# Modulation loads of a two-layer block spread over four stages instead of two

## The reference, cut to what matters

```python
c_act = jax.nn.silu(c)
for l in range(DEPTH):                      # DEPTH = 2
    mod = (c_act @ ada_w[l] + ada_b[l])[:, None, :]
    sh1, sc1, g1, sh2, sc2, g2 = jnp.split(mod, N_MOD, axis=-1)
    h = rms_norm(x, norm1_w[l]) * (1.0 + sc1) + sh1
    x = x + g1 * hybrid_mixer(h, w_in[l], w_out[l], ...)
    h = rms_norm(x, norm2_w[l]) * (1.0 + sc2) + sh2
    x = x + g2 * conv_ffn(h, w_gate[l], w_val[l], conv_w[l], conv_b[l], w_down[l])
return rms_norm(x, final_norm_w)
```

## Time and profile before

| | us |
|---|---|
| median of 3 runs | 4075.55 |
| lowest and highest of the 3 | 4073.48 and 4076.36 |
| the profiled execution, its own time | 4080.34 |
| its span in the trace | 4078.5 |
| granted TensorE clock, mean share of full | 0.978 |

### The profile page before, as it was taken

How to read it: one execution, slowest core, us unless ns; L and a number is a source line. 1 busy time by engine, 2 the same in 40 slices (tenths; PEclk the granted TensorE clock), 3 DMA queues, 4 the chain that set the end, 5 groups by cost and what they waited for, 6 DMA issues and landing times.

```text
span 4078.5 us, 69709 instructions
## 1 busy us (share of the span) xinstructions
PE 3851.0 (94%) x28924; PEld 3114.1 (76%) x28924; DVE 2019.9 (50%) x3575; ACT 1742.9 (43%) x2569; POOL 801.1 (20%) x1120
## 2 busy tenths in 40 slices
PE   8898999999899999999999999998999999989997
PEld 5676788777688877878777778876777788768885
DVE  4675662127543127256663466225545555356603
ACT  4365222347533247355553332235645554342223
POOL 1112222221222221200001222221120000222221
PEclk9899999999999999999999999999999999999998
DMA  9846998984589974833224789986573222779995
GB/s 311 245 104 128 291 286 187 203 181 106 119 186 193 190 165 111 188 72 68 68 64 97 168 181 195 190 179 143 114 174 68 62 57 55 155 155 194 190 194 133
DMA packets 191756, 628.98 MB, mean 154 GB/s; under 512 B 22993, under 2 KB 28369, under 8 KB 191057
## 3 DMA queue, kind: packets, MB, share of 16 engines
q0 software_dynamic: 160704, 549.53, 62.2%
q1 hardware_dynamic: 28176, 70.79, 5.0%
q10 hardware_dynamic: 2560, 4.20, 0.4%
HBM read 612.89 MB, written 2.10 MB: 151 GB/s over the span
## 4 chain that ended last, share of the span: by engine, by line
PE 48%; ACT 6%; DVE 5%; DMA 2%; issue 1%; SPq 0%; DVEq 0%; ACTq 0%; POOL 0%
PE bank L228 11%; PE bank L230 11%; PE bank L229 11%; PE bank L2081 6%; ACT gate L2241 1%; PE bank L1767 1%; PE bank L2044 1%; ACT L2241 1%; PE bank L2070 1%; DVE rw_z L2503 1%; PE bank L1749 1%; PE bank L1740 1%; ACT acc L2241 1%; DMA at_sw<-at_raw 1%; ACT w_lo L161 1%
## 5 line engine op out<-in xcount | busy, mean ns | idle before, releaser
L228 PE MATMUL bank<-h_hi,w_hi 128*128 128x512 f32 x2608 | 1068.2, 410 | 37.5 <-DMA w_lo<-in_b_wup 12.5
L230 PE MATMUL bank<-h_hi,w_lo 128*128 128x512 f32 x2608 | 1025.4, 393 | 0.0
L229 PE MATMUL bank<-h_lo,w_hi 128*128 128x512 f32 x2608 | 1024.8, 393 | 0.0
L161 ACT ACTIVATE w_lo<-w_hi 128x1024 fp32r<-128x1024 f32 (+2 forms) x558 | 557.0, 1002 | 1017.6 <-DMA w_hi<-in_a_wgv 297.3
L228 PEld LDWEIGHTS bank<-h_hi,w_hi 128*128 128x128 f32 x2608 | 495.1, 190 | 171.6 <-issue 54.8
L229 PEld LDWEIGHTS bank<-h_lo,w_hi 128*128 128x128 f32 x2608 | 495.9, 190 | 106.6 <-issue 11.3
L230 PEld LDWEIGHTS bank<-h_hi,w_lo 128*128 128x128 f32 x2608 | 494.7, 190 | 107.3
L2241 ACT ACTIVATE gate<-bank 128x512 f32<-128x512 f32 x96 | 57.3, 597 | 274.2 <-PE bank L2081 274.1
L228 PE MATMUL bank<-fb_y_hi,w_hi 128*128 128x512 f32 x352 | 137.2, 390 | 0.4 <-DMA w_lo<-in_b_wd 0.4
L228 PE MATMUL bank<-fa_y_hi,w_hi 128*128 128x512 f32 x352 | 137.0, 389 | 0.4 <-DMA w_lo<-in_a_wd 0.4
L230 PE MATMUL bank<-fb_y_hi,w_lo 128*128 128x512 f32 x352 | 137.0, 389 | 0.0
(11 more groups left out here) (462 smaller groups left out, 7566.3 us busy)
## 6 DMA issues: line engine op xcount, KB each, us to landing
w_hi<-in_a_wgv POOLq DMA_DIRECT2D x80, 512.0 KB, 5.6
w_lo<-in_a_wgv POOLq DMA_DIRECT2D x80, 512.0 KB, 7.7
w_hi<-in_b_wup POOLq DMA_DIRECT2D x80, 512.0 KB, 5.2
w_lo<-in_b_wup POOLq DMA_DIRECT2D x80, 512.0 KB, 7.4
w_hi<-in_a_wh POOLq DMA_DIRECT2D x48, 512.0 KB, 4.9
w_lo<-in_a_wh POOLq DMA_DIRECT2D x48, 512.0 KB, 5.6
fa_ada_raw<-in_ada SPq DMA_DIRECT2D x48, 512.0 KB, 8.2
w_hi<-in_b_wrkv POOLq DMA_DIRECT2D x48, 512.0 KB, 4.6
```

Source lines behind the costliest of these rows:

```text
L161: st.do(st.eng.activation(self.lo[:, s], self.hi[:, s].bitcast(F32), ACT.Copy, scale=-1.0), (self.neg_made, n + 1))
L228: pe.matmul(out, self.hi[:, a], hh[:, k0 + k, :], start=first and k == 0, stop=False)
L229: pe.matmul(out, self.hi[:, a], hl[:, k0 + k, :], start=False, stop=False)
L230: mm = pe.matmul(out, self.lo[:, a], hh[:, k0 + k, :], start=False, stop=last and k == ks - 1)
```

## The change

The work stays the same in kind and amount: 80 loads, 20 groups behind the prologue. It is divided otherwise:

| stage | loads before | loads after | groups after |
|---|---|---|---|
| mixer, layer 0 | 32 | 24 | 4 to 9 of layer 0 |
| feed-forward, layer 0 | 48 | 32 | 10 and 11 of layer 0, 0 to 5 of layer 1 |
| mixer, layer 1 | 0 | 16 | 6 to 9 of layer 1 |
| feed-forward, layer 1 | 0 | 8 | 10 and 11 of layer 1 |

Each feed-forward now makes the `g2` that it multiplies by at its own end. In the mixer of layer 0 the 16 loads after the early ones are added at 4 in a section (two at u = 0, one each at u = 1 and 2) instead of 6 (two each); in the mixer of layer 1 at 2 in a section (places 0, 1, 3, 4, 6, 7, 9, 10). In the feed-forwards 2 loads are added in a block instead of 3, in blocks 0 to 15 and 0 to 3. Products come behind projections 0, 0, 3, 6, 9, 12 in the first mixer (before: 0, 0, 2, 4, 6, 8, 10, 12) and 0, 0, 5, 11 in the second.

```diff
@@ mixer_a
-        ada = Ada(sc, run, [io["ada"][0, g, d] for g in range(4, 12) for d in range(4)]) if l == 0 else None
+        groups = range(4, 10) if l == 0 else range(6, 10)
+        ada = Ada(sc, run, [io["ada"][l, g, d] for g in groups for d in range(4)])
...
         def ada_at(d):
 
-            return (d - EARLY) // 2
+            return (d - EARLY) * 3 // (2 if l else 4)
...
-            if ada:
-                pe.wait_ge(mods_kept, 1)
+            pe.wait_ge(mods_kept, 1)
...
-                if ada and G == 5:
+                if G == 5:
                     dve.wait_ge(ada.used, ada.groups)
                     st.settle()
-                    at = A_AT["ada_b"][0]
-                    st.do(dve.tensor_tensor(mods[:, 0, 16:48], banks[7][:, 0:32], par[:, at + 16:at + 48], ALU.add),
-                          (mods_kept, 1))
+                    at, first, count = A_AT["ada_b"][0], 4 * groups[0], 4 * ada.groups
+                    st.do(dve.tensor_tensor(mods[:, l, first:first + count], banks[7][:, 0:count],
+                                            par[:, at + first:at + first + count], ALU.add), (mods_kept, 1))
@@ ffn_a
-        ada = Ada(sc, run, [io["ada"][1, g, d] for g in range(12) for d in range(4)], 3, raw, 4) if l == 0 else None
+        groups = [(l, 10), (l, 11)] + [(1, g) for g in range(0 if l else 6)]
+        ada = Ada(sc, run, [io["ada"][i, g, d] for i, g in groups for d in range(4)], 3, raw, 2 if l else 4)
...
         def ada_at(d):
 
-            return d // 3
+            return d // 2
...
-            if ada:
-                dve.wait_ge(ada.used, ada.groups)
-                st.settle()
-                at = A_AT["ada_b"][0]
-                st.do(dve.tensor_tensor(mods[:, 1, :], banks[7][:, 0:48], run.par_a[:, 1, at:at + 48], ALU.add))
+            dve.wait_ge(ada.used, ada.groups)
+            st.settle()
+            at = A_AT["ada_b"][0]
+            st.do(dve.tensor_tensor(mods[:, l, 40:48], banks[7][:, 0:8], par[:, at + 40:at + 48], ALU.add))
+            if l == 0:
+                st.do(dve.tensor_tensor(mods[:, 1, 0:24], banks[7][:, 8:32], run.par_a[:, 1, at:at + 24], ALU.add))
```

More of the change, by code:

```diff
@@ L809, in _ @@
             sp.dma_start(reset[:, :], io["a_reset"]).then_inc(const_in, 16)
-            for d in range(ada.steps if ada else 0):
+            for d in range(ada.steps):
                 ada.load(sp, d)
@@ L1101, in _ @@
                     ws.project(pe, banks[i % 2][:, :], hh, hl, between=between)
-                    for g in range(ada.groups if ada else 0):
+                    for g in range(ada.groups):
                         if max(ada_at(4 * g + 3), -1) + 1 == i:
@@ L1295, in _ @@
             st.do(dve.tensor_scalar(omlb[:, :], lbt[:, :], -1.0, 1.0, ALU.mult, ALU.add), (par_made, 1))
-            for d in range(EARLY if ada else 0):
+            for d in range(EARLY):
                 ada.add(st, d)
@@ L1418, in _ @@
             sc.enter_and_clear(sp)
-            if ada:
-                for d in range(ada.steps):
-                    ada.load(sp, d)
+            for d in range(ada.steps):
+                ada.load(sp, d)
             if rope:
```

## The result

The changed kernel took 4050.95 us (median of 4 runs, 4046.7 to 4051.45), the kernel before 4075.95 beside it (4 runs, 4073.48 to 4076.36). The ratio is 0.9941 with a 95% interval of 0.9929 to 0.9953, so the gain is 24 us (19 to 29). The prediction was 4069.5 us, a gain of 6. The sign was forecast, the size was not.

What follows compares the result with a forecast made beforehand. The prediction took TensorE, working in 94% of the span, to bound the kernel. Its terms -11, -7, +7.6 and +4.4 summed to -6.0 us, from a median of 4075.55 to 4069.5 us, range 4059 to 4080.

Steps and rivals of the forecast that it cites:

- First mixer: Layer 0 mixer, 32 to 24 loads and 8 to 6 groups: forecast to gain 11.2 us, taken as -11.
- upper bound of 22.8: First mixer, sections 0 to 3: largest gain in us if nothing but products remained, leaving 104.3 us.
- the replay: VectorE's in-order work in the first mixer, stepped through with measured durations to find which TensorE instructions wait next.
- the residue: First mixer, sections 0 to 3: 11.6 us of gaps, lower clock and late rotations still left after the change.
- gap at the scores of head 0: First mixer: scores due at 109.5, second rotation ready at 113.3; a 3.8 us gap replaces the product's 5.6.
- mask gap in section 3, with its clock: First mixer: value product waits 2.9 us for its mask in section 3, plus 1 us of lower clock.
- First feed-forward: Layer 0 feed-forward, 48 to 32 loads: four products less, -3.6, and fewer weight waits, -3.3; together -7 us.
- Second mixer: Layer 1 mixer, 0 to 16 loads: products +3.6, value projections +3, small gaps +1; together +7.6 us.
- rival (c): Second mixer's scores and value products fall behind VectorE in all four sections: +28 there, sum +14.6, 4090 us; chance 0.05.
- Second feed-forward: Layer 1 feed-forward, 0 to 8 loads: products +1.8, first weight wait +1.8, other loads 0.8; together +4.4 us.
- (b): First mixer's gaps go altogether, -20 there with the rest as forecast: sum -15, 4060.5 us; chance 0.2.
- (a): Each load costs its old average, 1.02 us in mixers, 0.45 in feed-forwards: sum +4.6, 4080 us; chance 0.2.

Runs made afterwards that it cites:

- the small loads: Kernel before, but modulation loads after those that first fill the slots bring 8 of 512 columns; additions and products stay: 4036.65 us, ratio 0.9914.
- the two versions with 24: Changed kernel with eight loads moved from first feed-forward to second mixer (24 each), with two or three load slots in the mixers: ratios 0.995 and 0.9946.
- three slots: Kernel before with three slots instead of two for the first mixer's loads, same loads in the same places: 4059.85 us, ratio 0.9973.

## Why the prediction was wrong

**First mixer, forecast -11, measured -17.4. This is the step that failed.** The upper bound of 22.8 and the floor of 104.3 us were near: TensorE is busy 104.70 us of the 109.26. The order of the replay was right as well. The gap of the product went, nothing waits for a product, the scores of head 0 are late next, and section 2's mask is late behind its pair (in the first of two executions). The stretch with sections 0 to 3 was forecast near 116 us and took 109.3 and 109.0. What failed is the residue, the time that the replay left in gaps and lower clock: 11.6 us forecast, 109.26 - 104.3 = 5.0 measured (4.7 in the second execution). Term by term:

| term of the residue | forecast | first execution | second |
|---|---|---|---|
| gap at the scores of head 0 | 3.8 | 1.48 | 2.07 |
| lower clock behind it | 2 | none | 1.4 |
| mask gap in section 2 | 1.6 | 0.88 | none |
| mask gap in section 3, with its clock | 2.9 + 1 | none | none |
| rotations late elsewhere | 1.3 | 1.32 | 0.18 |

(In the first execution 0.33 at section 1's mask, 0.55 of waiting for weights and 1.4 of longer busy time come on top; the forecast's 1.0 for the second mixer's own gap goes off.)

Two terms make nearly all of the difference, the scores of head 0 and the mask of section 3.

*Head 0.* The replay had the second transfer of the swap landed at 111.1, the rotation ready at 113.3 and TensorE there at 109.5. In the changed kernel that transfer (line 960, now 961) is issued at 104.0:

```profile
DMA to landing us min/median/max: 7.0/7.0/7.0
```

So it lands at 111.0 and the rotation ends at 113.1, as forecast; but TensorE gets there at 113.28 - 1.48 = 111.8. It began its first head projection 1.4 us later (89.92 against 88.50), and so the swap was issued 1.4 later too. Counted from that start, the landing is shorter by 1.5 us (7.0 for 8.5) and TensorE is later by 0.9, 0.55 of it a wait for weights. Together they turn 3.8 into 1.4. The 1.5 us are not shown to be the change's work. The loads up to here are the same ones before and after, and this transfer took 8.5, 7.3 and 7.8 us in three executions of the kernel before, 7.0 and 7.9 in two of the changed one. The forecast stood on the longest of the five.

*Section 3.* The prediction gives 2.9 + 1 without its working. The second load of this pair, issued at 162.4, landed sooner than the 6.2 of the earlier trace rows:

```profile
DMA to landing us min/median/max: 5.0/5.0/5.0
```

In the second execution it took 3.9 us. The swap that VectorE needs ahead of it (second rotation of section 2, issued at 154.0) took 4.5, and 4.6 in the second execution, where the median of the earlier trace rows is 6.6. My estimate from these rows: with 6.6 and 6.2 in place of 4.5 and 5.0 the load would be issued at 164.5, landed at 170.7 and added at 172.2, and the first mask made at 172.9, while the value product was due at 170.4. That is 2.5 us, near the forecast's 2.9. At this place landings were short whenever the loads were added four to a section: this swap took 4.5 to 5.2 us in seven executions, and 4.2 to 8.0 in six at six to a section.

Transfers in general did not become shorter. All second transfers of swaps in the first mixer, after the change:

```profile
DMA to landing us min/median/max: 4.5/6.7/7.5
```

The median is 6.7 here and 6.5 in the second execution; before it was 6.6, 5.9 and 6.6 in three executions. The loads issued from 100 to 191 us have medians of 6.0 and 6.0 after, and 6.2, 6.2 and 5.4 before. So a replay with one median for every transfer of a kind was wrong at single places and not by a common factor. The 5.3 us that it gives the swap of section 1 stand in no row; that swap took 7.0 and 4.8.

What did change is how long VectorE stands waiting for loads: 24.6, 18.7 and 23.0 us from 84 to 210 us in three executions of the kernel before, 10.0 and 13.1 in the changed one. With landings of the same length, I put this down to the larger distance between one addition and the next. That bytes in flight cause the gaps is shown by the small loads (332.9 us with all additions in place), and that the pace has a part of its own by six a section (339.6 against 334.2 with the same 24 loads). How much of the 6.4 us by which the forecast was off is the change's work and how much is scatter of single transfers stays open.

**The lower clock.** I took 2 us behind a gap of 3.8 and 1 behind 2.9. In the first execution, with gaps of 1.48 us at most, the clock stayed at its upper level, and the 8.1 us that I had put down to the clock went nearly whole: the stretch reads 1.00. In the second execution of the changed kernel the mechanism did show, smaller: a gap of 2.07 us ahead of the scores of head 0, and then eight matmuls in 3.82 us that take 2.39 otherwise:

```profile
114.20 3.82 PE L1012 MATMUL bank<-ma_rot 128*128 128x512 f32 x8 [2.07 <-DVE ma_rot L1202]
```

That is 1.4 us in place of 2, in a first mixer that still took 334.1. So a gap's price is its length plus what follows it, if anything does.

**First feed-forward, forecast -7, measured -9.2.** Four products less account for 3.6 at 0.9 each. The weight waits fell by 4.9 us in the trace (8.6 to 3.7), where I had said 3.3, and 0.7 is left over. The bound of -11 held. The choice of "perhaps a third" of the waits was a guess, and the rows had no better; most of the waits went, those at the start stayed, as said.

**Second mixer, forecast +7.6, measured +4.6.** The four products are there: sections 0 to 3 grew by 102.48 - 98.93 = 3.55 us, forecast 3.6. The value projections grew by 1.7 us, not 3: they took 46.94 against 45.23. I had carried over the difference between the first mixer and the second, less 1.5 for the chip's slow start. No run shows that 1.5. The first mixer's value projections take 51.63 us with the same eight loads, 4.7 more than these, so the difference between the two mixers is mostly something else and no measure of loads. The small gaps (+1) did not come; the slack of 2.66 us at the mask held. The stage's clock is 0.98, so rival (c) is out.

**Second feed-forward, forecast +4.4, measured +2.5.** Two products, 1.8, and 0.7 for the weight waits at the start, where I had 1.8 and 0.8.

**Sum.** The four terms were off by 6.4, 2.2, 3.0 and 1.9 us, all in one direction, 13.5 in all. No one cause for all four is shown. The first is the residue above, the third the value projections, and the second and fourth are no larger than the 2.3 us by which a feed-forward differs between executions of one kernel. The other 5 us are the difference between -19.5 in the stages of five executions and 24 by the medians, which is within the interval.

**Rivals.** (b), that the first mixer's gaps go altogether, was nearest to what happened: -17.4 where it said -20. It had 0.2; and even it kept the second mixer at +7.6 and gave 4060.5. The outcome is (b) together with a cheap second mixer, to which the prediction gave 0.05. Its own sign of being wrong, that the first mixer's gaps are gone, came true but for 4.0 us behind VectorE. (a), a load at its average price by kind of stage, was the farthest off. It said +4.6 and failed because a load has no such price. In the first mixer the loads from the 25th to the 32nd cost 17.4 / 8 = 2.2 us each, with their two products and the quicker pace of all late loads in it, and 12.0 / 8 = 1.5 at one and the same pace (six a section); those up to the 24th (334.2 - 323.2) / 24 = 0.46 on average, though that includes the start of the chip. In the feed-forward it is 9.2 / 16 = 0.58 a load from 48 down to 32, and (383.4 - 382.3) / 8 = 0.14 from 32 down to 24 (mean of the two versions with 24, which differ by 5 us from each other). In the second mixer it is 0.29 to 0.37 for sixteen, of which the product's share is 0.23, 0.63 for eight more. The change moves loads from the steep part of a curve to two flat ones.

**The rule.** The Trainium skill (DMA: Bandwidth & Descriptors, "Issuing engines are not separate DMA queues") says that transfers started by any engine share the 16 DMA engines and interleave. The second mixer agrees: the median of the swaps' second transfers was 4.4 to 4.5 us there in three executions without loads, 5.2 and 4.7 with two loads a section, and 6.5 with four. Its price is the prediction's +1 for small gaps, and that did not come. Between six and four loads a section in the first mixer the medians do not differ, as said.

**The range.** 4059 to 4080 was built on terms whose bounds I had written down: -23 to -6 in the mixer, -11 to -3.6, +3.6 to +15.6, +1.8 to +6.5. The outcome lies inside each of these. What shut it out was the weight: the low end was set at the likeliest case stretched over most of (b), and (b) with a cheap second mixer was left outside it.

## What to carry to other kernels

Background loads have no fixed price in this kernel: little more than their share of a product while they land ahead of their user, 1.5 to 2.2 us for each 512 KB load once the user stands waiting for them. A pair of like stages with and without them gives the average, which is too high for the flat part and too low for the steep one; look in the rows for the place where the user begins to wait.

When a replay moves a stall, its order may be right and its sizes wrong: this one leaned on one value for the swap that mattered, the longest of five executions, and on one median for transfers that in their places took 3.9 to 5.6 us. Take each term from several executions and at its own place, and carry the short and the long end through to the range. Before two runs are compared line by line, see that the line is the same: an inserted line moves all that follow, and of two transfers of one swap the second takes about 1 us longer here (medians of 5.7 and 6.6 us in the first mixer before). Moving only the instruction that waits gains nothing; what stands on the late engine ahead of it must get less.

Read one stage in several executions before its tenths are used: a stage that nobody had changed differed by 7.6 us between traces here, and the second block by 13.8.

## What the runs showed of the hardware

**The clock behind a gap does not follow from the gap's length.** The kernel before has 5.63 us of idle and then a product of 1.87 us (upper clock: 0.95), and 3.07 us and then a value product of 4.01 (2.32). With three slots a gap of 2.02 us was followed by the lower clock (eight matmuls in 4.12 us), one of 2.91 us later was not (2.39 us):

```profile
125.90 4.12 PE L1025 MATMUL bank<-ma_kept,ma_v_tok 128*128 128x512 f32 x8 [2.02 <-DVE ma_kept L1172]
```

```profile
179.13 2.39 PE L1025 MATMUL bank<-ma_kept,ma_v_tok 128*128 128x512 f32 x8 [2.91 <-DVE ma_kept L1172]
```

In the repeat of the kernel before a gap of 2.56 us left the product near its time at the upper clock, and in the third execution one of 2.54 us did not:

```profile
111.36 1.05 PE L496 MATMUL bank<-ones,ma_ada_rows 128*128 128x1 f32 x8 [2.56 <-DVE ma_ada_rows L488]
```

```profile
148.81 1.87 PE L496 MATMUL bank<-ones,ma_ada_rows 128*128 128x1 f32 x8 [2.54 <-DVE ma_ada_rows L488]
```

What decides between them was not found. In the first execution of the changed kernel the four gaps behind VectorE, 0.33 to 1.48 us, were all followed by eight matmuls in 2.39 to 2.44 us.

**An unchanged stretch scatters.** The second block took between 2583.4 and 2597.2 us in three executions of one kernel, and the first mixer 347.9 to 355.5; in the two executions of the changed kernel the first mixer, without its long gaps, took 334.3 and 334.1.
